# Seven block products for half of the gate and up products of the first feed-forward network, with their block sums on GpSimd

## The chip, the cores and the metric

The kernel runs on one NeuronCore of a Trainium2 chip. The metric is the device time of one execution in microseconds (us). TensorE (PE) multiplies into eight PSUM banks, VectorE (DVE) and ScalarE (ACT) read and write PSUM and SBUF, GpSimd (POOL) here does small arithmetic and some DMAs, and the queue of SyncE (SP) issues the DMAs of all weights.

## The reference

Two transformer blocks over 256 rows of width 2048 in fp32: attention and a feed-forward network, then sliding-window attention and a second feed-forward network. What is changed lies in the first feed-forward network, whose hidden width is 5632:

```
hn = rmsnorm(h, ffn_norm[l])
h = h + (jax.nn.silu(hn @ w_gate[l]) * (hn @ w_up[l])) @ w_down[l]
```

## The kernel before

All weights are streamed once, as 812 chunks. `weight_chunks` (L40) lists them in the order of use; a chunk is two k tiles (128 rows each) of 512 columns, 128x1024 in SBUF and 512 KB in DRAM. SP loads chunk t into one of four `raw` slots (`fetch`, L480) as soon as the chunk four places earlier has been split. Each fp32 chunk is split in two fp32r parts: ACT copies it to `whi` (`cast`, L600), DVE forms `wlo = raw - whi` (`subtract`, L903). The ring of `whi` and `wlo` has three slots, so `cast(t)` waits for PE to be done with chunk t-3. The left side (`Th`, `Tl`, or `Hh`, `Hl` for the hidden rows) is split in the same way, so that every product of a 128-row tile by 512 columns is three matmuls (`stream`, L1336): high by high, high by low, low by high (L1357 to L1359). With two k tiles and two halves of the 256 rows a chunk is 12 matmuls:

```
eng.matmul(o, lh[:, ts], hi[:, kk, :], start=start, stop=False)
eng.matmul(o, lh[:, ts], lo[:, kk, :], start=False, stop=False)
mm = eng.matmul(o, ll[:, ts], hi[:, kk, :], start=False, stop=stop)
```

The first feed-forward network has 11 column groups f of 512. For each the eight `gate` chunks come first, into one pair of banks, then the eight `up` chunks, into the other pair; ACT takes the silu of the gate banks to `SG` (L673), DVE multiplies the up banks with it to `HID` (L966), PE transposes `HID` (`htr`, eight transposes a group, L1399), and ACT and DVE split the transposed rows into `Hh` and `Hl` (`hsp`, L588 and L1155). Then `dn` (88 chunks) multiplies by `w_down`, one column group of 22 chunks after the other; DVE adds its banks to `X` (L960).

The order of the work beside the stream is written out by hand: `side_steps` (L115) puts each step at a chunk, and each engine runs through the chunks in order: ACT and DVE do the cast or the subtraction of chunk t+2, then the banks to be emptied, then the steps at t; PE does the 12 matmuls of t and then its steps. Banks 4 to 7 go in turn to the steps. POOL's queue holds the `pow` that makes each row's 1/rms (`row_rstd`, L525), two pairs of memsets and some loads; the `pow` number 3 belongs to the norm ahead of this network.

Of the kernel before, what the change touches and what calls it, by code (L numbers as in the profile page):

```python
# [28 lines left out]
TWO_PI = 2 * math.pi  # L29

# [9 lines left out]
def weight_chunks():  # L40
# [21 lines left out]
    nf = [(512 * i, 512) for i in range(NF)]  # L62
    for f in range(NF):
# [9 lines left out]
    for f in range(NF):  # L73
# [6 lines left out]


EMPTIED_BY = {"c": "AA", "qkv": "AA", "g": "AV", "uq": "AV", "ukv": "AV", "a": "VV", "b": "VV", "out": "VV",
              "gate": "AA", "up": "VV", "dn": "VV", "in2": "AA", "part": "AA", "post": "VV", "rest": "VV",
# [31 lines left out]
def side_steps():  # L115
# [57 lines left out]
    for v, t0, step in ((0, OUT, 8), (1, DN, 22)):  # L173
        for i in range(4):
            t = t0 + step * (i + 1)
# [5 lines left out]
        put(t0 + 4 * step + 1, "rs", 3 + v)  # L181
    for f in range(NF):
        t = FFN + 16 * f + 16
        for b in range(2):
            put(t + 1, "htr", 2 * f + b)
        for b in range(2):
            put(t + 2, "hsp", 2 * f + b)
# [26 lines left out]
    for g in range(2 * NF):  # L214
        for f in range(4):
            for j in range(3 if g % 2 == 0 else 5):
# [6 lines left out]
              "Ttr": 1, "htr": 1, "ktr": 1, "qtr": 1, "pscore": 2, "pptr": 2, "ppv": 1, "busy": 1, "row": 1}  # L223
# [42 lines left out]
def build(nc, A):  # L266
    ctx = ExitStack()
    with ctx:
# [37 lines left out]

        Hh = at("Hh", rH, 0, [FT, S], F32R)
# [53 lines left out]
        l_raw = sems("raw0 raw1 raw2 raw3")  # L361
# [16 lines left out]
        s_yhi, s_Y, s_mtr, s_mhi, s_M, s_htr, s_hhi, s_H = sems("yhi Y mtr mhi M htr hhi H")  # L378
# [14 lines left out]
        chunks = weight_chunks()  # L393
        first, last, order, banks, bank_before, emptied = groups_of(chunks)
# [25 lines left out]
        def side_freed(use):  # L420
# [24 lines left out]
            if name == "htr":  # L445
                return s_H, 2 * i + 2
# [30 lines left out]
        def sync_program(eng):  # L477
            sp = Seat(eng)

            def fetch(t):  # L480
                _, _, k0, a, n, name, c = chunks[t]
                if t >= RAW:
                    sp.wait_ge(s_lo, t - RAW + 1)
                out = raw[:, t % RAW, 0:a * n].rearrange("p (a n) -> p a n", a=a)
                eng.dma_start(out, w[name][:, k0:k0 + a, c:c + n]).then_inc(l_raw[t % RAW], 16)
# [32 lines left out]
        def gpsimd_program(eng):  # L518
# [11 lines left out]

            eng.dma_start(GT[:, :], A["gains_t"][:, 0:118]).then_inc(l_gains, 16)
# [20 lines left out]
            row_rstd(3)  # L552
# [3 lines left out]
            po.wait_ge(s_mm, DN)  # L556
            eng.dma_start(GB[:, :], bass.AP(A["final_norm"].tensor, 0, [[0, P], [1, D]])).then_inc(l_gf, 16)
            row_rstd(4)
            po.wait_ge(s_mm, IN2)
# [24 lines left out]
        def scalar_program(eng):  # L584
# [15 lines left out]
            def cast(t):  # L600
                _, _, _, a, n, _, _ = chunks[t]
                ac.wait_ge(l_raw[t % RAW], 16 * (t // RAW + 1))
                if t >= RING:
                    ac.wait_ge(s_mm, t - RING + 1)
                eng.copy(whi[:, t % RING, 0:a * n], raw[:, t % RAW, 0:a * n]).then_inc(s_cast, 1)  # L605
# [7 lines left out]
            def empty(g):  # L613
                st, i = g
                b = [bank[z] for z in banks[g]]
                if st not in ("post", "rest", "dn2"):
                    ac.wait_ge(s_mm, last[g] + 1)
# [49 lines left out]
                elif st == "gate":  # L667
                    ac.wait_ge(s_rs, 4)
                    if i:
                        for t in range(2):  # L670
                            ac.wait_ge(*emptied_at(("up", i - 1), t))
                    for t in range(2):
                        eng.activation(SG[:, t, :], b[t][:, :], ACT.Silu, scale=rs_2[:, t:t + 1]).then_inc(s_emptyA, 1)  # L673
# [16 lines left out]
                elif st == "part":  # L690
                    ac.wait_ge(s_mm, PART)
                    for t in range(2):
                        copy(PR[:, i - 2, t, :], b[t][:, :]).then_inc(s_emptyA, 1)
                elif st in ("post", "dn2"):
                    for t in range(2):
                        if t == 0:
                            ac.wait_ge(s_half, main_no[g] + 1)
                        else:
                            ac.wait_ge(s_mm, last[g] + 1)
                        square(b[t][:, :], 6 if st == "post" else 8, 4 * t + i)  # L700
# [5 lines left out]
            def side(name, i, t):  # L706
# [54 lines left out]
                elif name == "ysplit":  # L761
                    ac.wait_ge(s_y, 2 * i + 2)
                    ac.wait_ge(s_mm, G2 if i < 3 else BR)
# [11 lines left out]
                elif name == "Tsp":  # L775
                    ac.wait_ge(s_Ttr, i + 1)
                    ac.wait_ge(s_mm, (OUT, DN, PART)[i // 8])
# [5 lines left out]
                    for z in range(2):  # L783
                        k = 2 * (i % 8) + z
                        if 8 <= i < 16:
                            ac.wait_ge(s_gfn, 1)
                        copy(Th[:, k, :], b[:, z * S:(z + 1) * S], gain[:, g0 + k:g0 + k + 1]).then_inc(s_thi, 1)
                elif name == "hsp":
                    ac.wait_ge(s_htr, i + 1)
                    if i == 0:  # L790
                        ac.wait_ge(s_mm, FFN)
                    b = bank[side_bank["htr", i, 0]]
                    for z in range(2):
                        copy(Hh[:, 2 * i + z, :], b[:, z * S:(z + 1) * S]).then_inc(s_hhi, 1)
# [48 lines left out]
                elif name == "conv0":  # L843
                    st, f = conv_bank(i)
                    ac.wait_ge(s_mm, last[st] + 1)
# [18 lines left out]
            for t in range(END):  # L864
                if t + 2 < END:
                    cast(t + 2)
# [10 lines left out]
        def vector_program(eng):  # L877
# [25 lines left out]
            def subtract(t):  # L903
                _, _, _, a, n, _, _ = chunks[t]
                ve.wait_ge(s_cast, t + 1)
                eng.tensor_tensor(wlo[:, t % RING, 0:a * n], raw[:, t % RAW, 0:a * n],  # L906
                                  whi[:, t % RING, 0:a * n].bitcast(F32), ALU.subtract).then_inc(s_lo, 1)
# [11 lines left out]
            def empty(g):  # L919
                st, i = g  # L920
                b = [bank[z] for z in banks[g]]
                if st in ("c", "qkv", "gate", "part"):
                    return
                if st not in ("post", "rest", "dn2"):
                    ve.wait_ge(s_mm, last[g] + 1)
# [29 lines left out]
                elif st in ("out", "dn"):  # L955
                    for t in range(2):
# [3 lines left out]
                        eng.tensor_tensor(xs, b[t][:, :], xs, ALU.add).then_inc(s_emptyV, 1)  # L960
                elif st == "up":
                    if i >= 2:
                        ve.wait_ge(s_htr, 2 * (i - 2) + 2)
                    for t in range(2):
                        ve.wait_ge(*emptied_at(("gate", i), t))
                        eng.scalar_tensor_tensor(out=HID[:, i % 2, t, :], in0=b[t][:, :], scalar=rs_2[:, t:t + 1],  # L966
                                                 in1=SG[:, t, :], op0=ALU.mult, op1=ALU.mult).then_inc(s_emptyV, 1)
# [13 lines left out]
                elif st == "rest":  # L981
                    for t in range(2):
# [3 lines left out]
                        else:  # L986
                            ve.wait_ge(s_mm, last[g] + 1)
# [71 lines left out]
            def side(name, i, t):  # L1059
# [80 lines left out]
                elif name == "Tsp":  # L1140
# [3 lines left out]
                    for z in range(2):  # L1144
                        k = 2 * (i % 8) + z
                        ve.wait_ge(s_thi, 16 + 2 * i + 2)
                        eng.scalar_tensor_tensor(out=Tl[:, k, :], in0=b[:, z * S:(z + 1) * S],  # L1147
                                                 scalar=gain[:, g0 + k:g0 + k + 1], in1=Th[:, k, :].bitcast(F32),
                                                 op0=ALU.mult, op1=ALU.subtract).then_inc(s_T, 1)
                elif name == "hsp":  # L1150
                    b = bank[side_bank["htr", i, 0]]
                    for z in range(2):
                        k = 2 * i + z
                        ve.wait_ge(s_hhi, 2 * i + 2)
                        eng.tensor_tensor(Hl[:, k, :], b[:, z * S:(z + 1) * S], Hh[:, k, :].bitcast(F32),  # L1155
                                          ALU.subtract).then_inc(s_H, 1)
# [9 lines left out]
                elif name == "psoft":  # L1166
# [6 lines left out]
                    else:  # L1173
                        ve.wait_ge(s_mm, IN2)
# [101 lines left out]
            for t in range(END):  # L1276
                if t + 2 < END:
                    subtract(t + 2)
# [20 lines left out]
        def tensor_program(eng):  # L1299
            pe = Seat(eng)  # L1300

            def operand(st, k):
# [20 lines left out]
                if st == "dn":  # L1323
                    pe.wait_ge(s_H, k + 1)
                    return Hh[:, k, :], Hl[:, k, :]
# [10 lines left out]
            def stream(t):  # L1336

                st, i, k0, a, n, _, _ = chunks[t]
                g = (st, i)
                hi = whi[:, t % RING, 0:a * n].rearrange("p (a n) -> p a n", a=a)  # L1340
                lo = wlo[:, t % RING, 0:a * n].rearrange("p (a n) -> p a n", a=a)
                pe.wait_ge(s_lo, t + 1)
                if first[g] == t:
                    if st == "dn2":
                        pe.wait_ge(s_cv0, 84 if i < 2 else 88)
                    elif bank_before[g]:
                        for half in range(2):
                            pe.wait_ge(*emptied_at(bank_before[g], half))
                ends = last[g] == t
                for ts_ in ((0,), (1,)) if ends else ((0, 1),):  # L1350
                    for kk in range(a):
                        lh, ll = operand(st, k0 + kk)
                        start = first[g] == t and kk == 0
                        stop = ends and kk == a - 1
                        for half in ts_:
                            o, ts = bank[banks[g][half]][:, 0:n], slice(half * P, (half + 1) * P)
# [7 lines left out]
            def stream_t(t):  # L1364

                st, i, k0, a, n, _, _ = chunks[t]
                g = (st, i)
                hi = whi[:, t % RING, :].rearrange("p (a n) -> p a n", a=a)
                lo = wlo[:, t % RING, :].rearrange("p (a n) -> p a n", a=a)
                pe.wait_ge(s_lo, t + 1)  # L1370
# [30 lines left out]
            def side(name, i):  # L1401
# [103 lines left out]
                elif name == "htr":  # L1505
                    b = take("htr", i)
                    f = i // 2
                    for z in range(2):
                        c = (2 * (i % 2) + z) * P
                        for t in range(2):  # L1510
                            pe.wait_ge(*emptied_at(("up", f), t))
# [72 lines left out]
            for t in range(END):  # L1584
                if chunks[t][0] in ("gate2", "val2"):
                    stream_t(t)
                else:
                    stream(t)
                for name, i in steps[t]:
                    side(name, i)  # L1590
# [98 lines left out]
```

## Time and profile before

| | us |
|---|---|
| median of 3 runs (lowest to highest) | 2370.86 (2370.78 to 2371.09) |
| the profiled execution: device time | 2369.46 |
| its span, first to last instruction | 2367.7 |
| PE busy | 2346.6 |
| DVE busy | 1437.1 |
| ACT busy | 1149.5 |
| POOL busy | 23.9 |

The profiled execution lies 1.40 us below the median. Busy shares are means over the whole span. The spans of matmuls overlap one another, so the distance from one start to the next is the cost of one, not its duration.

### The profile page before, as it was taken

Reading aid. Unit: us, or ns where it says so; the run is one execution under the profiler, and the core shown is the slowest. Engines: PE = TensorE matmul, PEld = TensorE weight load, DVE = VectorE, ACT = ScalarE, POOL = GpSimd, SP = SyncE. Lnnn points to the kernel's source line nnn. Section 1 sums busy time; section 2 is a strip of 40 time slices with the busy share of each in tenths; the row PEclk is TensorE's granted clock in tenths of the full one; section 3 lists DMA queues with packets and bytes.
Section 4 is the critical chain, followed back from the end, with each engine's and each line's share of the span. In section 5 each row is a group of like instructions: output and inputs, shape, how many; then the busy total and the mean of one; then the engine's idle time right before and its main releaser. Section 6 shows DMA issues by size and latency. Waiting matters only on the chain.

```text
span 2367.7 us, 28497 instructions
## 1 busy us (share of the span) xinstructions
PE 2346.6 (99%) x11298; PEld 1963.7 (83%) x11298; DVE 1437.1 (61%) x2039; ACT 1149.5 (49%) x1704; POOL 23.9 (1%) x35
## 2 busy tenths in 40 slices
PE   8999999999999999999999999999999999999998
PEld 7888888888888888888888887788888888888886
DVE  6445565665554454454444566657888888885444
ACT  6445454545444444444444566655544444444442
POOL 1000000000000000000000100000000000000000
PEclk9999999999999999999999999999999999999999
DMA  7666555655666666666666665455666666666564
GB/s 261 187 187 175 156 174 152 186 185 181 195 187 189 193 188 188 193 188 205 191 191 190 209 197 163 131 151 179 188 193 189 189 193 188 189 193 191 192 194 151
DMA packets 226420, 439.25 MB, mean 186 GB/s; under 512 B 13632, under 2 KB 17888, under 8 KB 225904
## 3 DMA queue, kind: packets, MB, share of 16 engines
q1 hardware_dynamic: 224400, 429.51, 60.5%
q0 software_dynamic: 1888, 7.93, 1.1%
q8 instruction: 89, 1.46, 0.3%
q14 instruction: 43, 0.35, 0.0%
HBM read 435.24 MB, written 2.15 MB: 185 GB/s over the span
## 4 chain that ended last, share of the span: by engine, by line
PE 97%; ACT 1%; DVE 1%; issue 0%; DMA 0%; POOL 0%; DVEq 0%; ACTq 0%; POOLq 0%
PE bank L1357 24%; PE bank L1359 24%; PE bank L1358 24%; PE bank L1387 14%; PE bank L1389 7%; PE bank L1399 2%; PE bank L1543 1%; PE bank L1564 1%; PE bank L1442 0%; ACT whi L605 0%; PE bank L1459 0%; PE bank L1540 0%; PE bank L1565 0%; PE bank L1444 0%; ACT JK L597 0%
## 5 line engine op out<-in xcount | busy, mean ns | idle before, releaser
L906 DVE TENSOR_TENSOR wlo<-raw,whi 128x1024 fp32r<-128x1024 f32 (+1 forms) x812 | 988.1, 1218 | 883.3 <-ACT whi L605 882.6
L605 ACT CAST whi<-raw 128x1024 fp32r<-128x1024 f32 (+1 forms) x812 | 847.4, 1044 | 1158.7 <-PE bank L1359 907.0
L1357 PE MATMUL bank<-whi,TT 128*128 128x512 f32 (+1 forms) x1488 | 591.2, 397 | 3.2 <-DVE wlo L906 3.1
L1359 PE MATMUL bank<-whi,TT 128*128 128x512 f32 (+1 forms) x1488 | 578.2, 389 | 0.0
L1358 PE MATMUL bank<-wlo,TT 128*128 128x512 f32 (+1 forms) x1488 | 577.4, 388 | 0.0
L1387 PE MATMUL bank<-TT,whi 128*128 128x512 f32 x1408 | 488.9, 394 | 0.8 <-DVE TT L1147 0.7
L1389 PE MATMUL bank<-TT,wlo 128*128 128x256 f32 x1408 | 390.1, 277 | 0.0
L1357 PEld LDWEIGHTS bank<-whi,TT 128*128 128x128 f32 x1488 | 279.9, 188 | 62.1 <-DVE wlo L906 4.0
L1358 PEld LDWEIGHTS bank<-wlo,TT 128*128 128x128 f32 x1488 | 280.1, 188 | 58.1 <-issue 2.9
L1359 PEld LDWEIGHTS bank<-whi,TT 128*128 128x128 f32 x1488 | 279.6, 188 | 58.1
L1387 PEld LDWEIGHTS bank<-TT,whi 128*128 128x128 f32 x1408 | 264.0, 188 | 62.5 <-issue 1.3
L1357 PE MATMUL bank<-whi,Hh 128*128 128x512 f32 x704 | 274.3, 390 | 0.0
L1359 PE MATMUL bank<-whi,Hl 128*128 128x512 f32 x704 | 274.0, 389 | 0.0
L1358 PE MATMUL bank<-wlo,Hh 128*128 128x512 f32 x704 | 273.9, 389 | 0.0
L1389 PEld LDWEIGHTS bank<-TT,wlo 128*128 128x128 f32 x1408 | 264.3, 188 | 0.0
L1359 PEld LDWEIGHTS bank<-whi,Hl 128*128 128x128 f32 x704 | 132.1, 188 | 27.6
L1357 PEld LDWEIGHTS bank<-whi,Hh 128*128 128x128 f32 x704 | 132.2, 188 | 27.2
L1358 PEld LDWEIGHTS bank<-wlo,Hh 128*128 128x128 f32 x704 | 132.2, 188 | 27.2
L1357 PE MATMUL bank<-whi,YH 128*128 128x512 f32 x128 | 52.6, 411 | 0.0
L1357 PE MATMUL bank<-whi,MT 128*128 128x512 f32 x128 | 50.2, 392 | 0.0
L1359 PE MATMUL bank<-whi,YL 128*128 128x512 f32 x128 | 50.0, 391 | 0.0
L1359 PE MATMUL bank<-whi,MT 128*128 128x512 f32 x128 | 49.9, 390 | 0.0
(211 smaller groups left out, 1586.6 us busy)
## 6 DMA issues: line engine op xcount, KB each, us to landing
raw<-in_ffn_w_up_dram SPq DMA_DIRECT2D x176, 512.0 KB, 3.6
raw<-in_w_in_dram SPq DMA_DIRECT2D x120, 512.0 KB, 3.7
raw<-in_w_gate_dram SPq DMA_DIRECT2D x88, 512.0 KB, 3.7
raw<-in_w_up_dram SPq DMA_DIRECT2D x88, 512.0 KB, 3.7
raw<-in_w_down_dram SPq DMA_DIRECT2D x88, 512.0 KB, 4.7
raw<-in_ffn_w_down_dram SPq DMA_DIRECT2D x88, 512.0 KB, 4.8
raw<-in_swa_w_in_dram SPq DMA_DIRECT2D x48, 512.0 KB, 3.6
raw<-in_w_out_dram SPq DMA_DIRECT2D x32, 512.0 KB, 4.6
```

The lines of the kernel that those rows point to most:

```text
L605: eng.copy(whi[:, t % RING, 0:a * n], raw[:, t % RAW, 0:a * n]).then_inc(s_cast, 1)
L906: eng.tensor_tensor(wlo[:, t % RING, 0:a * n], raw[:, t % RAW, 0:a * n], whi[:, t % RING, 0:a * n].bitcast(F32), ALU.subtract).then_inc(s_ ...
L1357: eng.matmul(o, lh[:, ts], hi[:, kk, :], start=start, stop=False)
L1358: eng.matmul(o, lh[:, ts], lo[:, kk, :], start=False, stop=False)
L1359: mm = eng.matmul(o, ll[:, ts], hi[:, kk, :], start=False, stop=stop)
L1387: eng.matmul(o[:, :], hi[:, kk, fs], TT[:, k, :, :].rearrange("p a s -> p (a s)"), start=k == 0, stop=False)
L1389: mm = eng.matmul(o[:, 0:S], lo[:, kk, fs], Th[:, k, :], start=False, stop=k == KT - 1)
L1399: return eng.transpose(out, src, ident[:, :])
L1543: eng.matmul(b1[:, :], QP[:, c % 2, e, P:S], KK[:, g, :, :].rearrange("p a s -> p (a s)"), start=True, stop=True).then_inc(s_psc, 1)
L1564: eng.matmul(o[:, :], VV[:, 0, g, :, :].rearrange("p a e -> p (a e)"), pt[:, 0:512], start=True, stop=False)
```

## The change

For each group f, four of the eight pairs of k tiles (pairs 1 to 4, `SUMS`) are computed in another way. Such a cell takes one gate chunk and one up chunk. Seen as blocks it is a 2 by 2 (two halves of the rows, two k tiles) times a 2 by 2 (two k tiles, gate and up columns) product; before, it was eight block products of three matmuls, 24 in all, and now it is seven of three, by sums of blocks. The new steps of a cell in the stream are C (the gate chunk as it is, two block products), A (two sums of weight blocks, two products), B (two more sums, two products) and D (one block of the up chunk, one product). POOL forms the sums of weight blocks in three additions; ACT and DVE split C, A, B (128x1024 each) and D (128x512). Four sums of the blocks of the left side are made once per cell position, ahead of the network (`ex0` to `ex2`). Four banks collect products that gate and up share; at the end of a group DVE and ACT combine them (`one`, `sum`) and add them to the gate and up banks.

Further: gate and up chunks of the same pair now follow each other, in the order 1, 0, 2, 5, 3, 4 and then 6 and 7 of gate, 6 and 7 of up (first group: 0, 1, 5, 2, 3, 4); the network has four `whi`/`wlo` slots and three pairs of raw slots; silu runs in place on `SG`, the product `hid` in place on `HID`, one or two chunks later; `htr` of a group is done 12 chunks later; the hidden rows are kept whole in `HF`, and their splits are made in `dn`, one pair of k tiles at a time and once for each half of the columns (`form`, 44 times, 128x512 on ACT and on DVE), while `dn` takes two column groups at a time; `row_rstd(3)` stands behind the first cell's sums in POOL's queue.

```diff
+SUMS = (1, 2, 3, 4)
+ORDER0, ORDER = (0, 1, 5, 2, 3, 4), (1, 0, 2, 5, 3, 4)
...
     for f in range(NF):
-        product("gate", "w_gate", nf, KT, 0, [f])
-        product("up", "w_up", nf, KT, 0, [f])
-    product("dn", "w_down", n4, FT)
+        paired(("gate", f, "w_gate", 512 * f), ("up", f, "w_up", 512 * f), ORDER if f else ORDER0, (6, 7))
+    for h in range(2):
+        paired(*[("dn", i, "w_down", 512 * i) for i in (2 * h, 2 * h + 1)], range(18), range(18, 22))
...
+        if chunks[t][0] == "gate" and chunks[t][2] // 2 in SUMS:
+            rows += [("C", t), ("A", t), ("B", t), ("D", t + 1)]
...
+            def sums(n, t):
+                b = cell_raw(t)
+                t13 = TS13[:, n % 2, :].rearrange("p (a n) -> p a n", a=2)
+                t24 = TS24[:, :].rearrange("p (a n) -> p a n", a=2)
+                for z in (t, t + 1):
+                    po.wait_ge(l_raw[rslot[z]], 16 * raw_load[z])
+                if n >= 2:
+                    po.wait_ge(s_lo, step_of["A", cells[n - 2]] + 1)
+                eng.tensor_tensor(t13, b[:, 1:3, :], b[:, 3:4, :].to_broadcast([P, 2, 512]), ALU.add).then_inc(s_add, 1)
+                po.wait_ge(s_add, 3 * n + 1)
+                if n >= 1:
+                    po.wait_ge(s_lo, step_of["B", cells[n - 1]] + 1)
+                eng.tensor_tensor(t24[:, 0, :], t13[:, 0, :], b[:, 2, :], ALU.add).then_inc(s_add, 1)
+                po.wait_ge(s_add, 3 * n + 2)
+                eng.tensor_tensor(t24[:, 1, :], t24[:, 0, :], b[:, 0, :], ALU.add).then_inc(s_add, 1)
...
-            row_rstd(3)
+            for n, t in enumerate(cells):
+                if n == 1:
+                    row_rstd(3)
+                sums(n, t)
...
+            def subtract(u):
+                src = whole(u)
+                n = src.shape[-1]
+                ve.wait_ge(s_cast, u + 1)
+                eng.tensor_tensor(lo_at(u)[:, 0:n], src, hi_at(u)[:, 0:n].bitcast(F32), ALU.subtract).then_inc(s_lo, 1)
...
+                elif st == "gate":
+                    if i:
+                        ve.wait_ge(s_hd, 2 * i)
+                    ve.wait_ge(s_one, i + 1)
+                    eng.tensor_tensor(SG[:, 0, :], b[0][:, :], ST[:, 0, :], ALU.add).then_inc(s_emptyV, 1)
+                    ve.wait_ge(s_sum, 4 * i + 3)
+                    eng.tensor_tensor(SG[:, 1, :], b[1][:, :], ST[:, 1, :], ALU.add).then_inc(s_emptyV, 1)
...
+                        eng.tensor_tensor(HID[:, i % 2, t, :], b[t][:, :], ST[:, 2 + t, :], ALU.add).then_inc(s_emptyV, 1)
...
+                elif name == "sum":
+                    if part == 0:
+                        eng.tensor_tensor(u, q6[:, :], ST[:, 0, :], ALU.add).then_inc(s_sum, 1)
+                        eng.tensor_tensor(w_, q5[:, :], u, ALU.subtract).then_inc(s_sum, 1)
+                    else:
+                        eng.tensor_tensor(u, q7[:, :], u, ALU.add).then_inc(s_sum, 1)
+                        eng.tensor_tensor(z_, q5[:, :], u, ALU.subtract).then_inc(s_sum, 1)
...
+                if kind == "C":
+                    products = ((main(gate, 0), rows(even, 0)), (temporary(0), rows(odd, 0)))
+                elif kind == "A":
+                    products = ((temporary(1), sums_of_rows(1)), (temporary(2), sums_of_rows(3)))
+                elif kind == "B":
+                    products = ((temporary(3), sums_of_rows(2)), (main(gate, 1), rows(even, 1)))
+                else:
+                    products = ((main(("up", f), 0), sums_of_rows(4)),)
```

## Rows read from the trace of the kernel before

**Rows 1.** The page: busy time, and the chain that ended last by engine

```profile
PE 2346.6 (99%) x11298; PEld 1963.7 (83%) x11298; DVE 1437.1 (61%) x2039; ACT 1149.5 (49%) x1704; POOL 23.9 (1%) x35
...
PE 97%; ACT 1%; DVE 1%; issue 0%; DMA 0%; POOL 0%; DVEq 0%; ACTq 0%; POOLq 0%
```

**Rows 2.** Windows, one gate and up group each: width, busy us by engine, clock, DMA

```profile
656.44:700.86 44.42, 44.42 (x202) 36.87 (x201) 22.25 (x22) 19.04 (x22) 0.00 (x0) 1.00 0.65 190
700.86:745.27 44.41, 44.41 (x202) 36.84 (x201) 22.25 (x22) 19.04 (x22) 0.00 (x0) 1.00 0.64 189
```

**Rows 3.** The chain in order of time: a group's eight transposes (start, us)

```profile
700.86 0.87 PE bank L1399 x8
```

**Rows 4.** Instructions by form in 656.44:700.86: busy us, mean ns, idle before

```profile
L906 DVE TENSOR_TENSOR wlo<-raw,whi 128x1024 fp32r<-128x1024 f32 x16 | 19.6, 1225 | 22.2 <-ACT whi L605 22.2
L605 ACT CAST whi<-raw 128x1024 fp32r<-128x1024 f32 x16 | 16.8, 1048 | 25.4 <-PE bank L1359 25.4
L1155 DVE TENSOR_TENSOR Hl<-bank,Hh 128x256 fp32r<-128x256 f32 x4 | 1.4, 414 | 0.0
L966 DVE SCALAR_TENSOR_TENSOR HID<-bank,RS,SG 128x512 f32<-128x512 f32 x2 | 1.4, 744 | 0.0
```

**Rows 5.** Instructions by form, whole span: other shapes that price the new ones

```profile
L960 DVE TENSOR_TENSOR X<-bank,X 128x512 f32<-128x512 f32 x16 | 10.2, 682 | 0.0
L588 ACT ACTIVATE NAT<-bank,RS 128x512 f32<-128x512 f32 x20 | 12.6, 682 | 1.7 <-POOL RS L525 1.6
```

**Rows 6.** DVE in order of time, 1096 to 1104 (start, us): distance between starts

```profile
1096.46 1.23 DVE L906 TENSOR_TENSOR wlo<-raw,whi 128x1024 fp32r<-128x1024 f32 x1 [1.49 <-ACT whi L605]
1097.61 1.40 DVE L966 SCALAR_TENSOR_TENSOR HID<-bank,RS,SG 128x512 f32<-128x512 f32 x2
```

**Rows 7.** ACT and DVE behind PE's end of a chunk at 700.86 (start, us)

```profile
700.95 1.05 ACT L605 CAST whi<-raw 128x1024 fp32r<-128x1024 f32 x1 [1.68 <-PE bank L1359]
...
702.03 1.23 DVE L906 TENSOR_TENSOR wlo<-raw,whi 128x1024 fp32r<-128x1024 f32 x1 [1.50 <-ACT whi L605]
```

**Rows 8.** POOL in order of time: its memsets and arithmetic (start, us)

```profile
6.39 0.31 POOL L543 MEMSET KR<- 64x256 f32 x1
...
37.49 1.22 POOL L525 TENSOR_TENSOR RS<-MEAN,MHALF 128x2 f32<-128x2 f32 x1 [11.86 <-DVE MEAN L1004]
41.97 0.69 POOL L525 TENSOR_TENSOR RS<-MEAN,MHALF 128x2 f32<-128x2 f32 x1 [3.26 <-DVE MEAN L1004]
...
613.74 1.53 POOL L525 TENSOR_TENSOR RS<-MEAN,MHALF 128x2 f32<-128x2 f32 x1 [557.01 <-DVE MEAN L1004]
...
1345.50 1.54 POOL L525 TENSOR_TENSOR RS<-MEAN,MHALF 128x2 f32<-128x2 f32 x1 [249.01 <-DVE MEAN L1004]
1347.19 1.81 POOL L562 MEMSET KK<- 64x2048 f32 x1
```

**Rows 9.** DVE in order of time around those POOL instructions (start, us)

```profile
37.31 0.82 DVE L906 TENSOR_TENSOR wlo<-raw,whi 128x640 fp32r<-128x640 f32 x1
...
42.08 1.56 DVE L906 TENSOR_TENSOR wlo<-raw,whi 128x640 fp32r<-128x640 f32 x2 [0.26 <-ACT whi L605]
...
613.50 1.22 DVE L906 TENSOR_TENSOR wlo<-raw,whi 128x1024 fp32r<-128x1024 f32 x1
614.63 1.65 DVE L1147 SCALAR_TENSOR_TENSOR TT<-bank,GT,TT 128x256 fp32r<-128x256 f32 x4
...
1345.25 1.22 DVE L906 TENSOR_TENSOR wlo<-raw,whi 128x1024 fp32r<-128x1024 f32 x1
1346.38 1.65 DVE L1147 SCALAR_TENSOR_TENSOR TT<-bank,GFN,TT 128x256 fp32r<-128x256 f32 x4
```

**Rows 10.** Waits, 656 to 1095: engine, waited for, total us, times, longest

```profile
ACT whi L605 <- PE bank L1359: 250.5, 158, 2.0
DVE wlo L906 <- ACT whi L605: 220.3, 159, 1.8
```

**Rows 11.** DMA issues, 656 to 1095: KB each, median us to landing

```profile
raw<-in_w_up_dram SPq DMA_DIRECT2D x80, 512.0 KB, 3.7
```

More of the change, by code:

```diff
@@ L180, in side_steps @@
                 put(t + 2, "Tsp", 8 * v + 2 * i + b)
-        put(t0 + 4 * step + 1, "rs", 3 + v)
-    for f in range(NF):
[L183 to L187, printed above, removed]
+            for b in range(2):
+                if v == 0 and 2 * i + b in SUMS:
+                    for j in range(3):
+                        put(t + 3 + j, "ex%d" % j, SUMS.index(2 * i + b))
+        put(t + 1, "rs", 3 + v)
+    for f in range(NF):
+        tail = FFN + 16 * f + 12
+        if f == 0:
+            put(FFN + 1, "sq", f)
+        put(tail, "one", f)
+        put(tail, "sum", 2 * f)
+        put(tail + 1, "sum", 2 * f + 1)
+        if f:
+            put(tail + 2, "htr", 2 * f - 2)
+            put(tail + 3, "htr", 2 * f - 1)
+            put(tail + 3, "hsp", 2 * f - 2)
+            put(tail + 4, "hsp", 2 * f - 1)
+        put(tail + 3, "silu", f)
+        put(tail + 5, "hid", f)
+        if f < NF - 1:
+            put(tail + 3, "sq", f + 1)
+    for b in range(2):
+        put(DN + 3 + b, "htr", 2 * NF - 2 + b)
+        put(DN + 4 + b, "hsp", 2 * NF - 2 + b)
+    for j in range(44):
+        put(DN + 2 * (j - 3) if j > 2 else DN - 3 + j, "form", j)
     for c in range(4):
@@ L393, in build, with last_reader, raw_at, cell_raw @@
         chunks = weight_chunks()
+        work = weight_steps(chunks)
+        slot, slot_before = ring_slots(work)
+        rslot, raw_before, raw_load = raw_slots()
+        upto = [sum(z[1] < t for z in work) for t in range(END + 1)]
+        cells = [t for kind, t in work if kind == "C"]
+        step_of = {(kind, t): u for u, (kind, t) in enumerate(work)}
+        stands = {u: t for u, (kind, t) in enumerate(work) if kind in "wCD"}
+        def last_reader(t):
+            for kind in "wDB":
+                if (kind, t) in step_of:
+                    return step_of[kind, t]
+        def raw_at(t):
+            z = rslot[t]
+            return raw[:, z, :] if z < RAW else RX[:, z - RAW, :]
+        def cell_raw(t):
+            z = rslot[t]
+            pair = raw[:, z:z + 2, :] if z < RAW else RX[:, :, :]
+            return pair.rearrange("p c (a n) -> p (c a) n", a=2)
+        def hi_at(u):
+            return whi[:, slot[u], :] if slot[u] < RING else WX[:, 0, :]
+        def lo_at(u):
+            return wlo[:, slot[u], :] if slot[u] < RING else WX[:, 1, :]
+        def whole(u):
+            kind, t = work[u]
+            if kind == "A":
+                return TS13[:, cells.index(t) % 2, :]
+            if kind == "B":
+                return TS24[:, :]
+            return raw_at(t)[:, 0:512 if kind == "D" else chunks[t][3] * chunks[t][4]]
+        def ahead(u, c):
+            return c < len(work) and c <= u + RING and (slot_before[c] is None or slot_before[c] < u)
         first, last, order, banks, bank_before, emptied = groups_of(chunks)
@@ L844, in side @@
                     st, f = conv_bank(i)
[L845 removed]
+                    ac.wait_ge(s_mm, upto[last[st] + 1])
                     if i >= 3:
@@ L863, in scalar_program @@
             cast(1)
-            for t in range(END):
-                if t + 2 < END:
-                    cast(t + 2)
+            c = 2
+            for u in range(len(work)):
+                while ahead(u, c):
+                    cast(c)
+                    c += 1
+                if u not in stands:
+                    continue
+                t = stands[u]
                 if t + 2 < 8:
@@ L1275, in vector_program @@
             subtract(1)
-            for t in range(END):
-                if t + 2 < END:
-                    subtract(t + 2)
+            c = 2
+            for u in range(len(work)):
+                while ahead(u, c):
+                    subtract(c)
+                    c += 1
+                if u not in stands:
+                    continue
+                t = stands[u]
                 if t + 2 < 8:
@@ L1338, in stream @@
+            def stream(u):
+                t = work[u][1]
                 st, i, k0, a, n, _, _ = chunks[t]
                 g = (st, i)
[L1340 to L1348, printed above, removed]
+                hi = hi_at(u)[:, 0:a * n].rearrange("p (a n) -> p a n", a=a)
+                lo = lo_at(u)[:, 0:a * n].rearrange("p (a n) -> p a n", a=a)
+                pe.wait_ge(s_lo, u + 1)
@@ L1351, in stream @@
                     for kk in range(a):
-                        lh, ll = operand(st, k0 + kk)
-                        start = first[g] == t and kk == 0
+                        lh, ll = hidden(i, k0 + kk) if st == "dn" else operand(st, k0 + kk)
                         stop = ends and kk == a - 1
                         for half in ts_:
+                            start = begins(g, half)
                             o, ts = bank[banks[g][half]][:, 0:n], slice(half * P, (half + 1) * P)
@@ L1583, in tensor_program, with form_used @@
                 eng.matmul(bank[7][:, 0:P], ident[:, :], ident[:, :], start=True, stop=True)
-            for t in range(END):
-                if chunks[t][0] in ("gate2", "val2"):
-                    stream_t(t)
-                else:
-                    stream(t)
-                for name, i in steps[t]:
-                    side(name, i)
+            for u, (kind, t) in enumerate(work):
+                if kind != "w":
+                    stream_sums(u)
+                elif chunks[t][0] in ("gate2", "val2"):
+                    stream_t(u)
+                else:
+                    stream(u)
+                if u in stands:
+                    for name, i in steps[stands[u]]:
+                        side(name, i)
+        def form_used(j):
+            h, p = divmod(j, 22)
+            return DN + 44 * h + (2 * p + 1 if p < 18 else p + 22)
         PAIR_PARTS = ((0, 128), (128, 256), (256, 512), (512, 768))
```

265 lines of the change are left out of this document (202 added, 63 removed).

## Prediction, written before the changed kernel ran

> **What bounds the kernel now.** I read the page first: PE is busy for 99% of the span and carries 97% of the chain that ended last, while POOL is all but unused [rows 1]. Then the windows of two neighbouring groups of the gate and up products: 44.42 us each, PE busy throughout, DVE 22.25, ACT 19.04, POOL 0, clock 1.00 [rows 2]. Eight transposes take 0.87 us of it [rows 3], so 192 matmuls take 43.55, or 0.2268 us from one to the next. The other engines wait for PE: the cast for PE's banks, the subtraction for the cast, about 1.5 us a chunk [rows 10]. So here each matmul taken away is worth 0.2268 us, as long as ACT, DVE, POOL and the loads keep up. In the busy times of rows 4 I look for how far that is.
>
> **What the change takes away.** A cell has 21 matmuls in place of 24; four cells a group, 11 groups: 132 matmuls, 132 x 0.2268 = 29.9 us. A group becomes 180 x 0.2268 + 0.87 = 41.7 us for PE. Transposes and `dn` keep their counts. This is the most that can be won.
>
> **What DVE gets.** Per group it splits 8 plain chunks, C, A and B of four cells (12 more of 128x1024) and four D of 128x512. A subtraction's duration is 1225 ns [rows 4], but the next instruction starts 1.15 us after its start [rows 6]. For D the 640-column row gives 0.82 us [rows 9], so a column costs (1225 - 820) / 384 = 1.05 ns, 512 columns 0.69, and 0.62 from start to start. That is 20 x 1.15 + 4 x 0.62 = 25.5 us, where it was 16 x 1.15 = 18.4. Added are eight additions of a bank and an SBUF tile (four `sum`, two for gate, two for up), priced as the X addition, 682 ns [rows 5], some 0.65 from start to start: 5.2 us. The two multiplications `hid` stay at 0.7 each, 1.4 us [rows 6]; the four splits of `hsp`, 1.4 us [rows 4], leave for `dn`. Sum: 32.1 us of a 41.7 us group, 77%. By itself this fits. The worst place is a group's first cell: 3 x 1.15 + 0.62, two additions and `hid`, 6.8 us against PE's 21 x 0.2268 = 4.76; the plain pair behind it has 2.3 against 5.44. Over both that is 9.1 against 10.2, and the ring of four slots carries the 2 us between.
>
> ACT goes to 20 casts of 1.05, four of about 0.6, and five or six 128x512 instructions of at most 0.68 [rows 4, 5], some 27 us of 41.7: hidden behind PE. The sums of the left side, before the network, and the 44 `form` steps in `dn` (0.69 on DVE and as much on ACT per two chunks, or 5.44 us of PE, beside two subtractions of 1.23) cost nothing for the same reason; without PE in front of them `form` would cost 44 x 0.69 = 30 us. The loads are the same bytes, from 190 to 202 GB/s at most, landing in 3.7 us [rows 11] with three pairs in flight, some 15 us of PE work: nothing. `row_rstd(3)` now stands behind POOL's first cell, and only the silu some 30 us later waits for it: nothing.
>
> **Small waits.** At the start of `up` 0, of `dn` 1 and of `dn` 3, PE now needs a bank pair one chunk (2.72 us) after its last use; before, it had a group of 8 or 22 chunks in between. DVE frees the first half after the cast, the subtraction and one addition, (702.03 - 700.86) + 1.15 + 0.68 = 3.0 us after PE's end [rows 5, 7]. That is 0.3 us late, three times: 1 us, at worst 5 if queues are behind; below nothing is excluded, since each is an added wait. The combining chain at a group's end has two chunks, 5.4 us, until the next cell takes the gate banks: covered.
>
> **What POOL gets, and the door it shares.** This decides. A cell needs an addition of 1024 columns and two of 512, both inputs in SBUF. POOL has done nothing like it in this trace. What it shows is `pow` on two columns: 0.69 us where DVE began no subtraction of two SBUF tiles before it, but 1.22, 1.53 and 1.54 where one was running [rows 8]. In each of the three it ends 0.55 to 0.58 us after the end of the subtraction (613.74 + 1.53 = 615.27, against 614.72; 1347.04 against 1346.47; 38.71 against 38.13 [rows 9]). And it isn't hindered by the multiplications with one input in a bank that run from 614.63 and 1346.38. So POOL's reads wait for a DVE subtraction to be over: two-input DVE work and POOL's reads go through one door, one at a time. Whether DVE waits as long for POOL isn't seen: the subtractions at 42.08 began 0.11 us into a `pow` and took their usual 0.78 each, but two columns are read in no time. I take the door to be mutual.
>
> The Trainium skill ("SBUF — State Buffer", Who interferes with whom) says so: a DVE instruction with two SBUF inputs and a GpSimd instruction that reads SBUF exclude each other, and whichever is second waits for the whole of the first. By that rule the trace agrees with the one direction it can show, and the other speaks against this change.
>
> The price of an addition on POOL: the memsets give (1.81 - 0.31) / (2048 - 256) = 0.84 ns a column for one stream of data [rows 8]. An addition has three, two of them reads. Ends: 0.84 ns (all beside one another) and 2.5 (one after the other). As even the two-column arithmetic takes over twice as long as a 256-column memset, I take the middle between two and three streams, 2.1 ns: 2048 columns, 4.3 us a cell, 17.2 us a group, with the fixed part of each instruction outside the door. The skill ("GPSIMD Engine Reference", Elementwise — side-by-side cycle accounting) has 4497 ns for such an addition of 2048 columns; by it the group would have 18.0 us of POOL instead.
>
> **The sum.** Per group DVE's own 32.1 us and POOL's 17.2 can't overlap, save where DVE does the eight additions with a bank (5.2 us), of which I count half, 2.6, as met by POOL. Passing the door 12 times at about 0.1 us (estimate: the least distance seen between a release and the next start) adds 1.3. So 32.1 + 17.2 - 2.6 + 1.3 = 48.0 us, over PE's 41.7 and over today's 44.4. Eleven groups: 11 x 3.6 = +39.6 us; with the small waits +41. On the profiled execution's 2369.5 that is 2410.5; the median of the runs lies 1.4 higher, so 2412. POOL at 2.5 ns (20.6) gives 51.4 a group: +78, or 2449. PE would idle for 6 us a group, in pieces of 1 to 2 us; I expect the clock to stay at 1.00.
>
> **Rivals.**
> First, *DVE isn't held*: only POOL waits. DVE's 32.1 us then stay below 41.7, POOL's 17.2 and some 0.6 us of waiting twelve times a group, 24.4, too. The narrowest place is cell 4 right behind cell 3: from the subtraction of B to that of the next B two additions (2 x 1.1 and fixed parts), a cast and a subtraction, about 6 us, against PE's 4.76 plus 3 us of lead from the ring. PE stays fed, and the time is 2370.9 - 29.9 + 1 = 2342. For it: the undisturbed subtractions at 42.08, and PE's slack today. Against: the door that rows 8 and 9 show has no reason to favour one side. It decides as soon as DVE isn't held for over (41.7 - 32.1) = 9.6 us a group.
>
> Second, *held, but POOL's additions are cheap*: at two streams, 1.67 ns, POOL has 13.7 us and the group comes to 44.5: +1 to +2, no change, 2372; at one stream, 6.9 us, PE is the bound again and it is the first rival's time.
>
> Third, *POOL starves or grabs in the wrong order*: long additions of 2.2 us ahead of a subtraction that PE wants, and none of the additions meeting POOL's reads, gives 50.6 a group and more, 2440 to 2450; it lies on the forecast's side.
>
> That the change doesn't remove what it says is excluded by the count, 7 x 3 against 8 x 3.
>
> **Chances.** About 0.2%, 4.7 us, is what a measurement of this kernel can tell from no change. Forecast with the third rival: 0.60, slower. DVE not held: 0.30, faster. Cheap additions: 0.10, of which 0.08 no change and 0.02 faster. Both signs hold much, so the likeliest case has a range of its own, 2385 to 2450. The whole range reaches from just above the first rival's time, 2343, to the dear end of POOL's price, 2450.
>
> **What would show it.** Right: windows of a group at 46 to 50 us with PE busy well below the width; PE's waits on `wlo`; subtractions of 128x1024 whose mean grows from 1225 ns to 1.8 or more while POOL's additions are on; POOL busy 17 to 25 us a group. The first rival shows subtractions at 1225 ns, PE without gaps, a group of 41.7 us. Cheap additions show a 128x1024 addition below 1.9 us on POOL. A clock below 1.00, loads landing in over 6 us, or waits of several us at the three bank changes would make the prediction wrong in ways not priced here.

## The result, and the profile after

The changed kernel takes 2385.72 us (median of 4 runs, 2385.57 to 2387.08) against 2370.82 before: ratio 1.0065, 95% interval 1.0048 to 1.0083. It is slower, as forecast, but by 15 us and not by 41. The page of the changed kernel, busy time and the chain by engine:

```profile
PE 2334.9 (98%) x11166; PEld 1935.3 (81%) x11166; DVE 1703.5 (71%) x2235; ACT 1249.1 (52%) x1837; POOL 324.0 (14%) x167
...
PE 87%; DVE 9%; ACT 2%; issue 1%; POOL 1%; DMA 0%; DVEq 0%; ACTq 0%; POOLq 0%
```

The 132 matmuls are gone (11298 to 11166), and a tenth of the chain has gone over from PE to DVE [rows 1]. The windows of the changed kernel, the start of the network with its first group, and then one later group, transposes to transposes (width, busy us of PE, PEld, DVE, ACT, POOL, clock, DMA):

```profile
606.40:656.90 50.50, 44.29 (x187) 34.72 (x186) 46.35 (x39) 25.25 (x32) 27.69 (x14) 0.97 0.49 157
...
836.85:881.72 44.87, 42.97 (x191) 34.25 (x189) 42.75 (x35) 25.50 (x29) 28.03 (x13) 1.00 0.57 187
```

A group takes 44.9 us, where it was 44.4 [rows 2]: DVE is busy for 42.75 of it, PE is no longer full. From the first matmul of the network to the first of `dn` it is 503.4 us (606.62 to 1110.07) against 488.7: eleven groups at 0.5 more are 5.6 us, and 9 us more are lost in the first group. From `dn` on the kernel is 1.3 us longer, ahead of the network 0.2. Together 16, the difference of the two spans (2383.9 and 2367.7).

Where DVE's time goes shows in the order of time. First DVE, then POOL, of the changed kernel (start, duration):

```profile
839.63 2.32 DVE L1097 TENSOR_TENSOR wlo<-TS,whi 128x1024 fp32r<-128x1024 f32 x1 [1.07 <-ACT whi L772]
841.88 0.68 DVE L1097 TENSOR_TENSOR wlo<-raw,whi 128x512 fp32r<-128x512 f32 x1
842.48 1.27 DVE L1163 TENSOR_TENSOR HID<-bank,ST 128x512 f32<-128x512 f32 x2
843.68 1.21 DVE L1097 TENSOR_TENSOR WX<-raw,WX 128x1024 fp32r<-128x1024 f32 x1
844.81 2.32 DVE L1097 TENSOR_TENSOR wlo<-raw,whi 128x1024 fp32r<-128x1024 f32 x1
```

```profile
838.48 2.39 POOL L679 TENSOR_TENSOR TS<-RX 128x1024 f32<-128x1024 f32 x1
842.10 1.62 POOL L683 TENSOR_TENSOR TS<-TS,RX 128x512 f32<-128x512 f32 x1 [1.23 <-DVE wlo L1097]
843.79 2.25 POOL L685 TENSOR_TENSOR TS<-TS,RX 128x512 f32<-128x512 f32 x1
```

Both directions of the door are here. POOL's addition ends at 840.87, and the subtraction that began at 839.63 inside it ends 1.08 us later: it was held. The subtraction of 843.68 takes its usual 1.21, and POOL's addition of 843.79 takes 2.25 where it takes 1.30 undisturbed: POOL was held. The next subtraction, 844.81, then waits until POOL is out at 846.04 and ends 1.09 later. The addition of 842.10 first waits for the subtraction of 841.88, then runs beside the two additions from banks at 842.48, which keep their usual length.

Undisturbed, POOL takes 2.39 us for 1024 columns and 1.30 for 512 (the shortest of each line), so 2.13 ns a column and 0.21 fixed. The forecast took 2.1. The subtractions of a group at 836.85 to 881.72, the two commonest forms and the one held most:

```profile
L1097 DVE TENSOR_TENSOR wlo<-TS,whi 128x1024 fp32r<-128x1024 f32 x8 | 14.0, 1765 | 1.1 <-ACT whi L772 1.1
L1097 DVE TENSOR_TENSOR wlo<-raw,whi 128x1024 fp32r<-128x1024 f32 x6 | 10.6, 1800 | 0.9 <-ACT whi L772 0.8
L1097 DVE TENSOR_TENSOR WX<-RX,WX 128x1024 fp32r<-128x1024 f32 x2 | 4.5, 2226 | 0.0
```

All 21 subtractions of 128x1024 in this group have a mean of 1.72 us. They were 1225 ns [rows 4].

### The profile page after: what moved, and what is told of

Same layout as the page of the kernel before. It is cut to its first block, busy times and chain, and to the rows that moved or that the text cites. A ratio compares the mean times of both kernels' runs of the same rounds, so it can differ in the third digit from the quotient of the medians.

```text
span 2383.9 us, 28969 instructions
## 1 busy us (share of the span) xinstructions
PE 2334.9 (98%) x11166; PEld 1935.3 (81%) x11166; DVE 1703.5 (71%) x2235; ACT 1249.1 (52%) x1837; POOL 324.0 (14%) x167
## 4 chain that ended last, share of the span: by engine, by line
PE 87%; DVE 9%; ACT 2%; issue 1%; POOL 1%; DMA 0%; DVEq 0%; ACTq 0%; POOLq 0%
PE bank L1652 19%; PE bank L1654 19%; PE bank L1653 19%; PE bank L1683 14%; PE bank L1685 7%; DVE wlo L1097 6%; DVE WX L1097 2%; PE bank L1695 2%; PE bank L1631 1%; PE bank L1633 1%; PE bank L1632 1%; ACT whi L772 1%; PE bank L1839 1%; PE bank L1860 1%; PE bank L1738 0%
## 5 line engine op out<-in xcount | busy, mean ns | idle before, releaser
L1097 DVE TENSOR_TENSOR wlo<-raw,whi 128x1024 fp32r<-128x1024 f32 (+3 forms) x717 | 883.6, 1235 | 610.6 <-ACT whi L772 608.8
L772 ACT CAST whi<-raw 128x1024 fp32r<-128x1024 f32 (+3 forms) x717 | 734.4, 1026 | 898.2 <-PE bank L1654 630.0
L1652 PE MATMUL bank<-whi,TT 128*128 128x512 f32 (+1 forms) x1048 | 421.5, 402 | 9.5 <-DVE wlo L1097 7.6
L1654 PE MATMUL bank<-whi,TT 128*128 128x512 f32 (+1 forms) x1048 | 407.8, 389 | 0.0
L1653 PE MATMUL bank<-wlo,TT 128*128 128x512 f32 (+1 forms) x1048 | 407.2, 389 | 0.0
L1652 PEld LDWEIGHTS bank<-whi,TT 128*128 128x128 f32 x1048 | 197.5, 188 | 55.9 <-DVE wlo L1097 15.0
L1654 PEld LDWEIGHTS bank<-whi,TT 128*128 128x128 f32 x1048 | 197.5, 188 | 41.1
L1097 DVE TENSOR_TENSOR wlo<-TS,whi 128x1024 fp32r<-128x1024 f32 x77 | 138.3, 1809 | 11.1 <-ACT whi L772 10.7
L1652 PE MATMUL bank<-whi,FH 128*128 128x512 f32 x352 | 137.7, 391 | 0.4 <-DVE X L1150 0.4
L1654 PE MATMUL bank<-whi,FH 128*128 128x512 f32 x352 | 137.1, 389 | 0.0
L1653 PE MATMUL bank<-wlo,FH 128*128 128x512 f32 x352 | 137.0, 389 | 0.0
L1652 PE MATMUL bank<-whi,Hh 128*128 128x512 f32 x352 | 136.9, 389 | 0.0
L1654 PE MATMUL bank<-whi,Hl 128*128 128x512 f32 x352 | 136.9, 389 | 0.0
```

What stands on the lines that cost most here:

```text
L772: eng.copy(hi_at(u)[:, 0:src.shape[-1]], src).then_inc(s_cast, 1)
L1097: eng.tensor_tensor(lo_at(u)[:, 0:n], src, hi_at(u)[:, 0:n].bitcast(F32), ALU.subtract).then_inc(s_lo, 1)
```

## The experiments

All are edits of the changed kernel. Theory A is the forecast's: POOL's reads and DVE's two-input work exclude each other, both ways. First four runs, on what POOL's additions cost and how many cells a group can bear.

**Sums left out.** POOL's additions become memsets of the same tiles, so that gate and up are not the reference's.

```diff
-                eng.tensor_tensor(t13, b[:, 1:3, :], b[:, 3:4, :].to_broadcast([P, 2, 512]), ALU.add).then_inc(s_add, 1)
+                eng.memset(t13, 0.0).then_inc(s_add, 1)
...
-                eng.tensor_tensor(t24[:, 0, :], t13[:, 0, :], b[:, 2, :], ALU.add).then_inc(s_add, 1)
+                eng.memset(t24[:, 0, :], 0.0).then_inc(s_add, 1)
...
-                eng.tensor_tensor(t24[:, 1, :], t24[:, 0, :], b[:, 0, :], ALU.add).then_inc(s_add, 1)
+                eng.memset(t24[:, 1, :], 0.0).then_inc(s_add, 1)
```

> POOL's three additions a cell are left out (memsets of the same tiles stand in their place, 0.95 and 0.5 us), so the gate and up values are not the reference's; all waits, casts, subtractions and matmuls stay. Theory A (one door for POOL's reads and DVE's two-input work): a group falls from 44.9 us to PE's 41.7, subtractions of 128x1024 are back at 1.22 us, the time is 2342 to 2350. Theory B (DVE's own longer queue of 32 us and the latency of cast and subtraction starve PE, POOL does not matter): within 4 us of 2385.7.

2343.48 us, ratio to before 0.9886 (0.9871 to 0.9901).

**Writes nearly as long as the additions.** Each addition becomes two memsets in a row, 1.91 us for 1024 columns and 1.06 for 512 where the additions take 2.39 and 1.30; the sums are left out again. The edit of the first addition, where `fill` is a memset and the second one signals the end (the other two are changed in the same way):

```diff
-                eng.tensor_tensor(t13, b[:, 1:3, :], b[:, 3:4, :].to_broadcast([P, 2, 512]), ALU.add).then_inc(s_add, 1)
+                fill(t13, False)
+                fill(t13, True)
```

> Each of POOL's additions is replaced by two memsets of the same tile one after the other, which write only and take about as long (1.9 and 1.0 us against 2.4 and 1.3 undisturbed); the sums are left out, as above. Theory A: like the run without sums, within 4 us, subtractions at 1.22 us. Theory C (it is the time from raw chunk to sum, the cast waiting for POOL, not the reads): close to the changed kernel, 2375 to 2387, with subtractions at 1.22 us.

2343.27 us, 0.9885 (0.9870 to 0.9900). One group each, without the sums and then with the double memsets:

```profile
813.75:855.51 41.76, 41.76 (x190) 34.56 (x189) 33.01 (x35) 25.81 (x29) 7.78 (x12) 1.00 0.62 201
```

```profile
814.31:856.07 41.76, 41.76 (x190) 34.57 (x189) 33.00 (x35) 25.85 (x29) 16.20 (x25) 1.00 0.63 201
```

Both are PE-bound at 41.76 us a group, with PE full. The subtractions are back at their length; of the run with double memsets:

```profile
L1112 DVE TENSOR_TENSOR wlo<-TS,whi 128x1024 fp32r<-128x1024 f32 x46 | 56.2, 1223 | 10.9 <-ACT whi L787 9.1
```

POOL works for 16.2 us a group in the second and costs nothing. So it is neither DVE's longer queue (B) nor, up to four fifths of the additions' length, the time from raw chunk to sum (C), but what an addition does beyond a write: that costs 42 us (2385.7 - 2343.4). A memset leaves out the adding along with the two reads, and no run separates them; I call both the reads below. These runs also give what the rest of the change is worth, 27 us, and DVE's own work, 33.0 us a group.

**Three cells, two cells.**

```diff
-SUMS = (1, 2, 3, 4)
+SUMS = (1, 2, 4)
```

> Three cells a group in place of four (pairs 1, 2, 4), everything else as changed. Theory A: DVE's own 30.3 us and POOL's 13 us of reading no longer fill a group once a part meets the additions from banks; PE's 177 matmuls and transposes, 42.4 us (one cell fewer gives back 0.68), are the bound, and the time is 2355 to 2364, below the kernel before. Rival: a cell costs what it loses whatever their number, (44.9 - 41.7) / 4 = 0.8 us each; a group takes 44.8 and the time is 2380 to 2386.

2363.85 us, 0.9966 (0.9953 to 0.9979): faster than before. One of the five runs took 2356.92, the others 2363.65 to 2364.32; why is open. With `SUMS = (2, 4)`:

> Two cells a group (pairs 2 and 4). Theory A: PE-bound with slack, 43.1 us a group, 2360 to 2366, with hardly any wait of PE for a subtraction inside a group. Rival (constant loss a cell): 44.7 a group, about 2382.

2366.89 us, 0.9985 (0.9975 to 0.9995), at the upper edge and just above it. The loss isn't constant per cell. Two groups of the run with three cells:

```profile
737.42:779.89 42.47, 42.47 (x193) 35.09 (x192) 39.12 (x34) 24.28 (x27) 20.21 (x10) 1.00 0.61 199
865.00:909.85 44.85, 43.09 (x192) 34.87 (x191) 40.30 (x34) 24.07 (x27) 18.50 (x10) 1.00 0.59 187
```

Most groups are at PE's 42.4; three lose some 2.5 us. In the one shown PE finds the gate banks not yet freed (1.1 us of waiting for `SG`; a subtraction held to 3.36 us stands just ahead of the additions that free them) and one more subtraction late (0.7). With two cells a group takes 43.4 to 44.1, above PE's 43.1: pair 1 is plain there, so its up chunk wants both up banks one chunk into the group, and PE waited 4.6 us in all, 7 times, for `HID` to free them.

Then four runs on the size of the holds and on the first group.

**More reads.** Both 512-column additions are done twice.

```diff
+                eng.tensor_tensor(t24[:, 0, :], t13[:, 0, :], b[:, 2, :], ALU.add).then_inc(s_again, 1)
+                po.wait_ge(s_again, 2 * n + 1)
                 eng.tensor_tensor(t24[:, 0, :], t13[:, 0, :], b[:, 2, :], ALU.add).then_inc(s_add, 1)
```

> Each 512-column addition of POOL is done twice, 2.2 us more of reading a cell (8.7 a group of four cells), nothing else. Theory A (VectorE waits for each read; its additions from banks and its idle time, some 7 us a group, are already used up as cover): a group grows by 8 to 9 us, the time is 2470 to 2485. Rival (cover grows with POOL's share of the time, as two independent engines would meet): half of it, 2425 to 2440. If POOL were not the bound: 2386.

2506.0 us, 1.0575 (1.0561 to 1.0590): 120 us more, above theory A's range and far above the rivals'. Two groups:

```profile
842.61:898.98 56.37, 47.21 (x189) 36.14 (x189) 47.61 (x35) 25.09 (x30) 42.11 (x21) 0.94 0.44 150
898.98:954.29 55.31, 44.44 (x189) 33.87 (x189) 47.80 (x35) 24.98 (x30) 41.14 (x21) 1.00 0.45 152
```

A group grows by 10.9 us, that is 1.36 for each of the eight added instructions, a little over their undisturbed 1.30. DVE's busy time grows by 5 only; the other 6 us it is idle, and POOL is busy for 41 of 56: now the sums themselves come late (ACT waited 138 us in all for the last of them, 80 in the changed kernel), so that POOL's fixed 0.21 us and its own waits at the door count too. The clock has a part as well, which no run separates: it fell in seven of the nine groups between transposes, which take 55.5 to 57.3 us, and not in the other two, which take 54.8 and 54.9.

**A later start.** POOL's first sums wait for the end of the out product, and pairs 0 and 5 go first.

```diff
-ORDER0, ORDER = (0, 1, 5, 2, 3, 4), (1, 0, 2, 5, 3, 4)
+ORDER0, ORDER = (0, 5, 1, 2, 3, 4), (1, 0, 2, 5, 3, 4)
...
+                if n == 0:
+                    po.wait_ge(s_mm, upto[FFN])
```

> Four cells. POOL's first sums wait for the last chunk of the out product, and the first group takes pairs 0 and 5 ahead of its four cells. If the 9 us that the first group lost come from POOL's first sums holding the last subtractions of the out product and the left side's sums: 2377 to 2381. If they come from the changed order itself (up 0 beginning one chunk after out 3): no change, 2384 to 2388.

2384.91 us, 1.0061 (1.0047 to 1.0075): no gain, in the range that was to speak for the changed order. But the edit only moves the hold: POOL's first addition now falls on the subtraction ahead of the X additions (PE still waits 1.6 us for them), and the four cells in a row lose 4.8 us of PE time between 621 and 655. So it doesn't decide where the first group's loss comes from; the run without sums, which keeps the order, does. There the network takes 461.0 us from its start to `dn`, 1.6 over eleven groups of 41.76, where the changed kernel has 9 over eleven of its own. So the reads again, for 7 to 8 us.

**Three cells, each followed by a plain pair, and the later start.** `SUMS = (1, 2, 4)`, orders (0, 5, 1, 3, 2, 4) and (1, 0, 2, 3, 4, 5), and the wait above.

> Three cells a group, each followed by a plain pair (1, 0, 2, 3, 4, 5), and the later start. Theory A with PE as the bound: 42.4 us a group in all eleven and 2 us at the start, 2350 to 2358; if the single late subtractions seen with three cells come from the door alone and not from the order, 2360 to 2364.

2372.3 us, 1.0008 (0.9999 to 1.0017): a miss. It is 8 us slower than three cells in the given order. Its groups take 43.1 to 45.2, though in the shortest DVE is less busy (36.4 us); PE waited 16 times, 10.7 us in all, for the subtractions of plain chunks. Which part of the edit does it wasn't taken apart.

**Shorter reads.** The 1024-column addition as two of 512.

```diff
-                eng.tensor_tensor(t13, b[:, 1:3, :], b[:, 3:4, :].to_broadcast([P, 2, 512]), ALU.add).then_inc(s_add, 1)
+                eng.tensor_tensor(t13[:, 0, :], b[:, 1, :], b[:, 3, :], ALU.add)
+                eng.tensor_tensor(t13[:, 1, :], b[:, 2, :], b[:, 3, :], ALU.add).then_inc(s_add, 1)
```

> Four cells, the 1024-column addition made as two of 512: the same reads in holds of 1.1 us in place of 2.2. Theory A, by the sum of reads: 2383 to 2388 (a fixed 0.2 us a cell lies outside the door). Rival (the length of one hold decides, as a subtraction that PE wants comes behind it): 2365 to 2378, with fewer waits of PE for a subtraction.

2387.0 us, 1.0071 (1.0057 to 1.0085): with four cells the sum of the reads counts, not the length of one.

**The sums on DVE.** If DVE stands still while POOL adds, it might as well add. The three additions go into DVE's queue, the first ahead of the subtraction of C, two behind it; POOL does none.

```diff
             def subtract(u):
+                cell = cells.index(work[u][1]) if work[u][0] == "C" else None
+                if cell is not None:
+                    first_sums(cell, work[u][1])
                 src = whole(u)
                 n = src.shape[-1]
                 ve.wait_ge(s_cast, u + 1)
                 eng.tensor_tensor(lo_at(u)[:, 0:n], src, hi_at(u)[:, 0:n].bitcast(F32), ALU.subtract).then_inc(s_lo, 1)
+                if cell is not None:
+                    other_sums(cell, work[u][1])
```

> Four cells. The three additions of weight blocks move from POOL to VectorE, around the subtraction of C; POOL does none. VectorE takes 1.15 + 2 x 0.62 = 2.4 us a cell for them, where it is now held for 10.7 us a group of four, 2.7 a cell. Theory A: VectorE's own 32.1 + 9.6 = 41.7 us a group, as much as PE's; with what doesn't fit within a cell 42.5 to 43.5, the time 2354 to 2368, below the kernel with POOL's sums and the kernel before. Rival (POOL's help is worth having, since 20 us of additions a group can't move to the fuller engine without cost): 2390 or more.

2351.95 us, 0.9922 (0.9909 to 0.9936): below both kernels, with all four cells, and 2 us below theory A's range. A group of it, and its additions:

```profile
861.58:903.82 42.24, 42.07 (x190) 34.46 (x189) 41.64 (x47) 25.98 (x29) 0.00 (x0) 1.00 0.59 200
```

```profile
L1080 DVE TENSOR_TENSOR TS<-raw 128x1024 f32<-128x1024 f32 x20 | 24.3, 1217 | 0.0
L1089 DVE TENSOR_TENSOR TS<-TS,raw 128x512 f32<-128x512 f32 x20 | 13.7, 683 | 0.0
```

DVE carries everything in 41.64 busy us, 1.1 less than it was busy when POOL did the additions. The group is 2.6 us shorter; the other 1.5 were DVE's idle time, 2.1 us then and 0.6 here. With `SUMS = (1, 2, 4)` as well:

> The same with three cells a group (pairs 1, 2, 4). VectorE's own 30.3 + 7.2 = 37.5 us against PE's 42.4: PE is the bound in every group, 11 x 2.0 us less than before and some 2 us of small waits: 2349 to 2355. If the order of the steps costs what it did with three cells and POOL (single late subtractions): 2358 to 2364.

2352.92 us, 0.9928 (0.9914 to 0.9941), in the first of the two ranges. A group takes 42.47 us there, so that of the 0.68 us that PE gains by the fourth cell 0.23 comes through, as DVE's queue is full; over the whole kernel it is 1 us, less than can be told.

## Why the prediction was right and wrong

The direction and its mechanism held. PE's part was right: 132 matmuls, 0.2268 us each, a group at 41.76 once nothing else binds, and the first rival's time of 2342 is what the kernel does when the reads are gone (2343.4). POOL's price was right (2.13 ns a column against 2.1), with luck: 2.1 was the middle between two guesses from memsets. The door works both ways, as the prediction took from the one direction seen, and as the Trainium skill has it ("SBUF — State Buffer", Who interferes with whom). That page has the holder keep the other out for its whole instruction; here a two-column `pow` of 0.69 us did not hold the subtraction that began 0.11 us into it [rows 8, 9]. The first rival fell with the 2.32 us subtractions, cheap additions with POOL's 2.39 us. The small waits were about right: 1.3 us beyond the network.

What failed is one step of the sum, how much of POOL's 17.2 us DVE feels: "of which I count half, 2.6, as met by POOL", 1.3 us on top for twelve passages, and DVE's idle time counted as no cover. Measured on a group: DVE's own busy time is 33.0 us (the run without sums; forecast 32.1), busy time with the sums 42.75, so 9.7 us of being held, and DVE is idle for 2.1. Together 44.87, against 48.0. Beyond its own work that is 11.8, where the forecast had 17.2 - 2.6 + 1.3 = 15.9.

Where POOL's reading went can be laid over DVE's rows of the same group. I take the last 2.18 us of an addition of 1024 columns and the last 1.09 of one of 512 as its reading, 17.4 us in all. Of this 4.4 lie under DVE's additions from banks (5.4 there, so four fifths and not half) and 1.8 under its idle time (of 2.1). The other 11.2 lie beside work with two SBUF inputs, and lengthen it by 9.7 only: the held subtractions above end 1.08 and 1.09 us after POOL, where one takes 1.22 alone. So the passages, which the forecast had as a cost of 1.3, gave back 1.5. They are the larger part of the miss, the cover under the additions from banks (4.4 against 2.6) the smaller; DVE's idle time about outweighs its own cover. A likely reason for the cover is that POOL's next addition often stands at the door already (POOL is busy for 28.0 us a group with 20.0 of undisturbed work, so it waits for 8.0), and slips in with the first DVE instruction that leaves the door free, as the one of 842.10 does. That this is the cause is read from the trace; no run changed the amount of cover alone.

Eleven groups made +5.6 us instead of +39.6. In the other direction the forecast missed the first group: 9 us, against 0.3 for its bank wait. Of this 7 to 8 go away without the reads. Three rows of DVE there:

```profile
602.07 2.88 DVE L1362 TENSOR_TENSOR EX<-XS,EX 128x512 fp32r<-128x512 f32 x1
607.12 2.31 DVE L1097 TENSOR_TENSOR wlo<-raw,whi 128x1024 fp32r<-128x1024 f32 x1
616.60 2.36 DVE L1097 TENSOR_TENSOR wlo<-raw,whi 128x512 fp32r<-128x512 f32 x1 [1.39 <-ACT whi L772]
```

POOL's first cell is 601.20 to 608.34, still in the out product, and holds the subtractions of its last chunks and the splitting of the left side's sums, so that the additions to X come late and PE waits 1.8 us for them, 0.4 in the run without sums. The second cell's first addition (616.01 to 618.40) holds the third row, and PE waits 1.8 for the splitting of the normed rows behind it, against 0.25. I had priced the sums of the left side at nothing "behind PE", without asking what POOL would do in that stretch.

The stated range, 2385 to 2450, holds the measured 2385.7 by less than 1 us. Its lower end was worked out from no term, so this is luck: the sum was 26 us too high, and would have been 34 too high without the first group. Of the signs named, a group of 46 to 50 us and POOL busy for 17 to 25 did not come (44.9 and 28.0), and the clock did fall once, to 0.97 over the first group's window.

## What to carry to other kernels

An addition moved from DVE to GpSimd to relieve DVE did not relieve it here, where most of DVE's work has two SBUF inputs: count GpSimd's reading time as DVE's, less most of what DVE does with PSUM inputs or not at all. Here DVE was held for 2.4 us a cell (9.7 / 4) beside what the reads cost at the start, and did the same additions itself in 2.2 (41.64 - 33.0, over 4), with the kernel 34 us faster. When two engines share a door and one of them is often waiting at it, take most of the cover there is, then look separately at the places without cover, such as the stage in which the new work first starts.

## What the runs showed of the hardware that was not expected

A pause of PE of about 2 us at the start of the network was followed by a lower clock in the changed kernel. PE's last matmul before it began at 609.11, the next at 611.31. From 612.5 to 615.9 a 512-column matmul of the chain takes 0.43 us where it took 0.23; the window has a mean granted clock of 0.57, so most of it at the lower of the two levels, 1.2 GHz, and the next window is back at 1.00:

```profile
612.00:616.00 4.00, 4.00 (x14) 3.04 (x13) 1.47 (x3) 1.71 (x4) 0.65 (x1) 0.57 0.01 2
616.00:620.00 4.00, 2.23 (x14) 1.69 (x13) 3.40 (x4) 3.08 (x6) 3.92 (x3) 1.00 0.45 131
```

That is eight matmuls at up to 0.2 us more, 1.5 us of the first group's loss. The three-cell run has the same pause (PE waited the same 1.8 us for its X additions) and no such fall, and so has the run with shorter reads, at 1.00 from 612 to 620. That run and the one with the later start fell later, to 0.66 and 0.58 over 664 to 668, behind two waits of PE of 1.0 to 1.2 and 0.7 us; the three-cell run has two such waits as well, 1.0 and 0.7 between 657 and 661, and no fall. The length of a pause alone doesn't tell whether the clock falls.

And an engine in front of PE can be all but full: with the sums on DVE it is busy for 41.64 of 42.24 us, and PE, which waits for each of its subtractions, loses only 0.5 us a group to it (42.24 against 41.76).
